# The first head stage of a two-block kernel: from unsplit fp32 chunks to three split passes

## The reference

```python
h = modulate(rms_norm(x, norm_mix_g), shift, scale)   # [1, 256, 2048]
z = h @ w_in                                          # columns: q, k, v (8 heads x 128), u (1024), ...
y_sb = stick_breaking_attention(q, k, v)              # per head: softplus, cumulative sum, exp, weights @ v
y_s5 = s5_layer(u, ...)                               # complex linear recurrence over the 256 tokens
```

## Time and profile before

| what | us |
|---|---|
| median of two runs | 3001.72 (3000.17 to 3003.26) |
| the profiled execution | 2994.33 |
| its span, first to last instruction | 2992.5 |
| TensorE busy | 2746.7 |
| VectorE busy | 1427.4 |
| ScalarE busy | 1198.2 |
| GpSimd busy | 1699.4 |
| mean granted TensorE clock | 0.966 |

### The profile page before, as it was taken

The page is one execution under the profiler, slowest core; times in us unless marked ns, Lnnn a source line. Parts: engine busy times, 40 slices in busy tenths (PEclk is TensorE's granted clock), DMA queues, the critical chain, the costliest instruction groups (busy, mean ns, idle before and its releaser), DMA issues.

```text
span 2992.5 us, 49963 instructions
## 1 busy us (share of the span) xinstructions
PE 2746.7 (92%) x19154; PEld 2329.1 (78%) x19154; DVE 1427.4 (48%) x2212; ACT 1198.2 (40%) x1474; POOL 1699.4 (57%) x1281
## 2 busy tenths in 40 slices
PE   6899979999999999768888889799999999999998
PEld 1688868999998889624344369699989999998998
DVE  1388854446554586512222255277612443317344
ACT  1233334434455344301112035466544456645443
POOL 0000038988786898200000019777699987779998
PEclk8899989999999999889999999899999999999999
DMA  9533337778344879499999935434355554445543
GB/s 386 232 119 126 127 125 280 273 284 295 141 155 154 297 258 367 175 418 421 420 410 418 421 133 184 158 142 159 114 195 185 184 184 154 156 153 184 185 169 141
DMA packets 107840, 679.54 MB, mean 227 GB/s; under 512 B 12608, under 2 KB 16704, under 8 KB 34240
## 3 DMA queue, kind: packets, MB, share of 16 engines
q1 hardware_dynamic: 83088, 602.97, 53.3%
q10 hardware_dynamic: 24624, 74.73, 7.1%
HBM read 769.92 MB, written 2.10 MB: 258 GB/s over the span
## 4 chain that ended last, share of the span: by engine, by line
PE 75%; DMA 11%; DVE 4%; ACT 3%; POOL 3%; issue 2%; SPq 1%; ACTq 0%; POOLq 0%; DVEq 0%
PE acc L634 46%; PE acc L709 10%; PE wk L634 10%; DMA ring<-in_moe 6%; PE acc L713 5%; PE acc L722 3%; POOL w_lo L606 3%; DMA stage<-in_ada 2%; DMA side_buf<-in_ada 1%; DMA stage<-in_main 1%; ACT w_hi L1418 1%; ACT L1418 1%; PE wk L722 1%; SPq L556 1%; ACT X_ysb L1418 0%
## 5 line engine op out<-in xcount | busy, mean ns | idle before, releaser
L606 POOL TENSOR_TENSOR w_lo<-stage,w_hi 128x512 fp32r<-128x512 f32 x1264 | 1675.3, 1359 | 864.3 <-ACT w_hi L1418 531.2
L1418 ACT ACTIVATE w_hi<-stage 128x2048 fp32r<-128x2048 f32 x316 | 602.7, 1908 | 122.1 <-DMA stage<-in_main 115.7
L634 PE MATMUL acc<-xhl,w_hi 128*128 128x256 f32 x3904 | 497.6, 286 | 10.6 <-DVE C_raw L2780 5.7
L634 PEld LDWEIGHTS acc<-xhl,w_hi 128*128 128x128 f32 x3904 | 483.4, 194 | 11.6 <-DVE C_raw L2780 5.9
L709 PE MATMUL acc<-xhl,w_hi 128*128 128x512 f32 x1536 | 370.8, 394 | 6.0 <-ACT w_hi L1418 6.0
L709 PEld LDWEIGHTS acc<-xhl,w_hi 128*128 128x128 f32 x1536 | 285.4, 190 | 61.8 <-issue 6.2
L634 PE MATMUL acc<-xhl,w_lo 128*128 128x256 f32 x1952 | 259.2, 286 | 2.0 <-POOL w_lo L606 2.0
L634 PEld LDWEIGHTS acc<-xhl,w_lo 128*128 128x128 f32 x1952 | 244.3, 193 | 5.4 <-issue 2.5
L634 PE MATMUL acc<-h,stage 128*128 128x256 f32 x1024 | 235.9, 386 | 2.9 <-ACT h L1418 2.9
L626 POOL MEMSET over_end<- 128x4096 f32 x1 | 3.5, 3512 | 396.0 <-PE acc L634 396.0
L634 PEld LDWEIGHTS acc<-h,stage 128*128 128x128 f32 x1024 | 192.8, 192 | 39.7 <-issue 15.1
(11 more groups left out here) (508 smaller groups left out, 4065.0 us busy)
## 6 DMA issues: line engine op xcount, KB each, us to landing
stage<-in_main SPq DMA_DIRECT2D x317, 1024.0 KB, 4.8
ring<-in_moe SPq DMA_DIRECT2D x192, 1024.0 KB, 10.8
side_buf<-in_ada ACTq DMA_DIRECT2D x128, 512.0 KB, 6.2
over_lo<-in_moe ACTq DMA_DIRECT2D x46, 1024.0 KB
over_hi<-in_moe ACTq DMA_DIRECT2D x41, 1024.0 KB
stage<-in_ada SPq DMA_DIRECT2D x32, 1024.0 KB, 8.6
stage<-in_sb SPq DMA_DIRECT2D x32, 1024.0 KB, 4.8
over_end<-in_moe ACTq DMA_DIRECT2D x3, 1024.0 KB
```

Of the source, the lines that this page charges most:

```text
L606: last = pool.tensor_tensor(w_lo[:, k % 2, cs], stage[:, k, cs], w_hi[:, k, cs].bitcast(F32), ALU.subtract)
L634: return pe.matmul(o, w, r, start=start, stop=stop)
L1418: return act.activation(o, i, f, **kw)
```

## The change

The 32 chunks become the first phase of "main" (`("sb", N_SB)` at the head of `PHASES`), so that `high`, `low`, `chunk` and `step` treat them as all others: 48 fp32r matmuls in place of 16 in fp32, one copy on ScalarE and four subtractions on GpSimd per chunk. `h32` and the counters `sb_done` and `sb_evac` go; waits on them become waits on `evac_done`. All later chunks have numbers higher by 32, in the same buffers. VectorE now makes the modulated input in place in `hb`, all 16 tiles before it begins `split_lo`; ScalarE makes the first `high` ahead of the copies to `xh`, and three more after them. The constants `A_tri` and the first S5 matrices are loaded behind those.

```diff
-PHASES = [("p_sb", 8), ...
+PHASES = [("sb", N_SB), ("p_sb", 8), ...
@@ sync
-            sp.dma_start(stage[:, k, :], dr["sb"][k]).then_inc(load[k], 16)
-        with sp.Fori(1, SB_TURNS) as i:
-            for k in range(4):
-                sp.wait_ge(sb_done, i * 4 + (k - 3))
-                sp.dma_start(stage[:, k, :], dr["sb"][i * 4 + k]).then_inc(load[k], 16)
-        for k in range(4):
-            sp.wait_ge(sb_done, N_SB - 3 + k)
             sp.dma_start(stage[:, k, :], dr["main"][k]).then_inc(load[k], 16)
@@ gpsimd
-        pool.wait_ge(sb_done, N_SB)
-        pool.wait_ge(rms_lo, 4)
         for k in range(4):
             low(k, 0)
@@ tensor: plain(j, g, work)
-            pe.wait_ge(load[j], (g + ADA_TURNS) * 16 + 16)
-            pe.wait_ge(sb_evac, g * 4 + (j + 1))
-            for t in range(DT):
-                ...
-                last = mm(acc[:, j, 0:T], stage[:, j, t * P:(t + 1) * P], h32[:, t, :], t == 0, t == DT - 1)
-            last.then_inc(sb_done, 1)
+            wide(*slot(BASE["sb"] + j, g), mid=work, split=0 if isinstance(g, int) and g + j == 0 else None)
@@ scalar, ahead of the stage
-        act.wait_ge(mod_ready, 2)
-        fn(vtmp[:, 10:11], ones[:, 0:1], ACT.Copy).then_inc(sb_evac, 4)
-        for g in range(4):
-            act.wait_ge(rms_scaled, 1 + g)
-            for t in range(4 * g, 4 * g + 4):
-                fn(h32[:, t, :], hb[:, t, :], ACT.Identity, scale=a1[:, t:t + 1], bias=mod[:, t:t + 1]).then_inc(rms_affine_done, 1)
+        high(0, 0)
         for g in range(4):
             act.wait_ge(rms_affine_done, 4 * g + 4)
-            fn(xh[:, 4 * g:4 * g + 4, :], h32[:, 4 * g:4 * g + 4, :], ACT.Copy).then_inc(rms_hi, 1)
+            fn(xh[:, 4 * g:4 * g + 4, :], hb[:, 4 * g:4 * g + 4, :], ACT.Copy).then_inc(rms_hi, 1)
+        for k in range(1, 4):
+            high(k, 0)
+        act.wait_ge(rms_lo, 4)
         act.dma_start(A["tri"][:], dr["tri"]).then_inc(constA_in, 16)
         load_s5(0)
@@ scalar: evict and stage_a
-            act.wait_ge(sb_done, g * 4 + (j + 1))
-            fn(o, acc[:, j, 0:T], ACT.Identity).then_inc(sb_evac, 1)
+            step(j, g, to(o, j))
...
-                if g is None:
-                    for k in range(4):
-                        high(k, 0)
@@ vector, ahead of the stage
-        split_lo(h32, 0)
+        dve.wait_ge(mod_ready, 2)
+        for t in range(DT):
+            ts(hb[:, t, :], hb[:, t, :], a1[:, t:t + 1], MUL, mod[:, t:t + 1], ADD).then_inc(rms_affine_done, 1)
+        split_lo(hb, 0)
```

More of the change, by code:

```diff
@@ L53 @@
 N_SB = 32
-PHASES = [("p_sb", 8), ("g_sb", 8), ("glu", 4), ("g_sb2", 8), ("p_s5", 8), ("g_s5", 16), ("mlif", 1),
+PHASES = [("sb", N_SB), ("p_sb", 8), ("g_sb", 8), ("glu", 4), ("g_sb2", 8), ("p_s5", 8), ("g_s5", 16), ("mlif", 1),
           ("ml", 32), ("p_ml", 8), ("g_ml", 16), ("wout", 16), ("router", 1), ("kv", 12), ("bf", 1), ("cmp", 8), ("nsa", 32), ("p_a", 8), ("g_a", 16), ("p_b", 8), ("g_b", 16),
@@ L167, in build @@
     assert top[0] == B0 + (RING + 2) * CH * 4
-    h32 = sb("h32", [P, DT, T], at=top[0] - 2 * CH * 4)
     x = sb("x", [P, DT, T])
@@ L357, in build @@
     chunk_done = nc.alloc_semaphore("chunk_done")
-    sb_done = nc.alloc_semaphore("sb_done")
-    sb_evac = nc.alloc_semaphore("sb_evac")
     evac_done = nc.alloc_semaphore("evac_done")
@@ L479, in build @@
     ADA_TURNS = NADA // 4
-    SB_TURNS = N_SB // 4
     C0_D = 32
@@ L815, in bu @@
                 if j == 0:
-                    pe.wait_ge(sb_evac, s * 4 + 8)
+                    pe.wait_ge(evac_done, s * 4 + 4)
                     pe.wait_ge(s5_in, s * 32 + 32)
@@ L832, in stage_a @@
             if s is not None:
-                pe.wait_ge(sb_evac, s * 4 + 7)
+                pe.wait_ge(evac_done, s * 4 + 3)
                 pe.wait_ge(yl_ready, s + 1)
@@ L871, in _ @@
         heads(pe, stage_a)
-        pe.wait_ge(sb_evac, N_SB + 4)
+        pe.wait_ge(evac_done, N_SB)
         pe.wait_ge(yl_ready, 9)
@@ L955, in _ @@
         k, q = slot(BASE["router"])
-        pe.wait_ge(load[k], (q + ADA_TURNS + SB_TURNS) * 16 + 16)
+        pe.wait_ge(load[k], (q + ADA_TURNS) * 16 + 16)
         pe.wait_ge(evac_done, BASE["router"] - 3)
@@ L1425, in high @@
         def high(k, q):
-            act.wait_ge(load[k], (q + (ADA_TURNS + SB_TURNS)) * 16 + 16)
+            act.wait_ge(load[k], (q + ADA_TURNS) * 16 + 16)
             fn(w_hi[:, k, :], stage[:, k, :], ACT.Copy).then_inc(hi_ready, 1)
@@ L2204, in stage_a @@
             stt(A["cm"][:, :, 1, :], A["c2"][:, :, 0, :], -1.0, A["c1"][:, :, 1, :], MUL, SUB).then_inc(cm_ready, 1)
-            dve.wait_ge(sb_evac, s * 4 + 8)
+            dve.wait_ge(evac_done, s * 4 + 4)
             ts(A["du"][:], A["u"][:], vcol("s5_d", s), MUL).then_inc(du_ready, 1)
@@ L3046, in _layout @@
     w = i["w_in"][0]
-    a["sb"] = _tiles(interleave(w, [(0, P), (1024, P), (2048, P), (3072, P)], 8), DT)
+    put("sb", interleave(w, [(0, P), (1024, P), (2048, P), (3072, P)], 8))
     put("ml", interleave(w, [(4096, 256), (5120, 256), (6144, 256), (7168, 256)], 4))
```

## The result

The changed kernel takes 3075.73 us (3075.51 to 3075.95), the kernel before 3001.72: a ratio of 1.0256 [1.0231, 1.0281]. The forecast was 3096 us with a range of 3050 to 3122. Direction and mechanism came as forecast. The rise is 74 us where 94 were forecast, mainly because the largest term, the time for which GpSimd holds VectorE, was a quarter too large.

A forecast was written before the change was run, and what follows sets the result against it. TensorE was taken to set the head stage, with VectorE close behind and the bound after the change. Turns +100, last head -9.8 and start +4 gave +94 on 3001.7, so 3096 us, range 3050 to 3122.

The forecast's parts named there:

- no hit: Head stage: no GpSimd subtraction holds a VectorE instruction, so a head takes 33.7 us.
- Part 1, the matmuls: Head stage: split passes cut TensorE's work from 36.2 to 30.9 us a head, leaving VectorE to set it at 33.7.
- The cap of 2.5 us a head: Head stage: most that faster matmuls can gain before VectorE sets the head, 18 us over seven turns.
- The not-slower rival: Head stage: subtractions slip into VectorE's pauses and PSUM products; -23 us, 2978 us with none held; chance 0.05.
- Part 2, the stall: Head stage: GpSimd's new subtractions hold VectorE 15 times at 1.12 us, head 50.5 us, +100 us over seven turns.
- the low end: Head stage: 10 held VectorE instructions at 0.98 us, 43.5 us a head, +45 and 3047 us in all.
- bursts 1, 2 and 4: GpSimd's four-subtraction groups at tables, at small A_c, A_cm, A_du instructions, and in rotation 2: 4, 4 and 3 hits.
- Burst 3: GpSimd's third group of four subtractions in a head: falls into rotation 1 (scan, products, A_srot), 4 hits.
- Part 3, the end: Last head of the stage: w_hi copies made a head earlier remove waits, 27.9 us against 37.7, -9.8 us.
- Part 4, the start: Start of the stage: VectorE makes all 16 tiles before splitting; first A_zm near 137.7 against 133.93, +4 us.
- The clock rival: Head stage: TensorE's clock falls in its new pauses and stays down; 61.8 us a head, 3175 us; chance 0.03.
- Half the hits: Head stage: only 8 of 16 subtractions hold VectorE; 42.7 us a head, 3041 us; chance 0.11.

The follow-up runs named there:

- the first experiment: Changed kernel with GpSimd subtracting only 16 columns of each of the 32 head chunks, zeros written by memsets for the rest: 2980.33 us, ratio 0.9939.

## Why the prediction was right, and where its sizes were off

**Direction and mechanism.** VectorE became the bound, held by GpSimd's reads of SBUF. Both halves are shown: without the reads most heads take 34.1 us (forecast for "no hit": 33.7), with the reads alone, in the old kernel, 45.5. Half of the reads give about half of the loss.

**Part 1, the matmuls.** Right. TensorE's busy time is 31.76 us in a head at full clock (forecast 30.9); in the changed kernel, at a clock of 0.89, it is 34.7 to 35.5, so TensorE is idle for 12 to 13 us and not for 20. The cap of 2.5 us a head holds: without the reads 2.1 are gained in most heads. The not-slower rival, 2978 us "with no hit", comes close to the 2980.33 of the first experiment, but in part by luck: against the trace before, its turns give -11.4 us and not -17.5 (the last one still meets subtractions), its last head -7.9 and not -9.8, its start -2.7 and not +4.

**Part 2, the stall: this is the term that was mis-sized.** 15 hits of 1.12 us were forecast, +16.8; it was 13 of 0.98, +12.7.
- The size: 1.12 was taken from the `hb` products of 1024 columns; the row for a product of 256 columns, like most of those held here, gives 1393 - 412, 0.98. It stood in the text as the low end, and was the better value for wide instructions too: the held tables of 1024 columns lose 0.94 to 0.98 us (2.17 and 2.20 against 1.23, 1.67 and 1.66 against 0.69).
- The number (bursts numbered as in the prediction): bursts 1, 2 and 4 made 4, 4 and 3 hits as walked. Burst 3 was to fall into rotation 1 with four hits; it fell into the wait for `bu(2)` and the PSUM products of rotation 2, and made two. The walk had left out what part of a rival named, TensorE's low clock after its pause: it makes chunk 1 late and with it the burst. "A clock that is low for part of a head costs nothing while VectorE is the bound" was nearly right: it cost the wait of 1.2 us named next, and it saved two hits, about 2 us; the TensorE kept busy through its pause shows the burst in the other place.
- A wait was left out that takes some of this back: 1.22 us before `bu(2)`. So the head is 32.8 + 0.94 + 12.7 + 1.2 = 47.6, measured 47.8, forecast 50.5. Seven turns: +82.4 us where +100 was forecast.

**Part 3, the end.** -9.8 forecast, -8.9 measured; no wait of 8 us is left in the last head. The difference is the 0.90 us that VectorE waits for `bu(2)` at 490.76, which was not in the sum. That such a gain lasts isn't given: made by itself in the kernel before, it brought nothing, once through a new lock and once through the later stretch. In the changed kernel the early copies and bursts make it last until the stage's end; its further way can't be told from scatter.

**Part 4, the start.** +4 forecast, +1.8 measured. The first pass began at 109.54 (forecast 109.5), and three chunks took 17.3 as forecast; chunk 0 took 8.0, not 10, as the clock rose within it (0.50 until 114, 1.00 from 116 on). That the `hb` instructions took 8.04 us where 3.2 + 4.5 = 7.7 were forecast was luck. With GpSimd idle, in the run in which VectorE makes the low halves, the same 16 take 5.26, 0.33 each and not 0.2:

```profile
99.87 5.26 DVE L2007 TENSOR_SCALAR hb<-hb,a,mod 128x256 f32<-128x256 f32 x16
```

So their own time was put 2.1 us too low and the holding, 2.8 us in all, 1.7 too high. The start scatters by 3 us between executions of the kernel before, so this term is below what the runs can tell.

**The sum.** +94 forecast, +74.0 by the medians (+76.8 on the second chip). Against the forecast, the turns came out 17.6 us lower, the end 0.9 higher and the start 2.2 lower. (The low end of the prediction's own sum, 3047 us, lies outside its stated range of 3050 to 3122.)

The clock rival (3175 us) failed as its own counter-argument said: the clock is low for some 10 us of a head, and only the wait of 1.2 us comes of it. Half the hits (3041 us) was not far from the truth in its place, as burst 3 did fall on PSUM products, but for one burst of four.

## What to carry to other kernels

Before work goes to an idle GpSimd beside a dense VectorE, count how many of VectorE's instructions have two SBUF operands or are long scalings: in this kernel each one met cost most of the length of GpSimd's instruction, and the same work on VectorE itself was cheaper (42.7 us a head against 47.8 here). VectorE's busy share doesn't warn: holding is booked as work, and shows only in the mean of one form beside the same form with an operand in PSUM. And walk the bursts along the other engine's order: which instructions they fall on decides as much as how many there are.

## What the runs showed that was not expected

- The lock is lopsided. In one head VectorE loses 12.7 us, while GpSimd's four bursts take 23.7 us against 4 x 5.06 undisturbed: 3.5 lost.
- GpSimd's writes alone hold little, and not always VectorE. In the trace without the reads, pairs `A_vr` beside memsets take 0.76 to 0.79 us (0.76 free). Of the scalings `A_cos<-A_ph`, 0.69 us free, one beside memsets takes 2.44 (at 114.16) and one 1.18 (at 198.23), but others 0.71, and there the four memsets take 2.45 in place of 1.91.
- Keeping TensorE busy through its longest pause moved its slow stretch and didn't remove it, and brought no gain: the chunk that ended sooner sent its burst onto four of VectorE's instructions instead of two.
- Repeated profiles of an unchanged kernel differ by 12 us in one stretch of 260, with totals only 8 apart: a difference of a few microseconds far behind a change is to be held against that first.
